# The S5 half of the first output projection moved into attention, two score areas instead of three, and a later turning and router

## What the reference computes

```python
s = jnp.einsum('bqhcd,bkhcd->bchqk', q_blk, k) * scale
p = jax.nn.softmax(jnp.where(mask, s, NEG_INF), axis=-1)
w = p[:, 0] - lam * p[:, 1]
return jnp.einsum('bhqk,bkhe->bqhe', w, v)
...
return jnp.concatenate([y_s5, y_da], axis=-1) @ w_out.astype(F32)
```

## Time and profile before

| what | value |
|---|---|
| median of three runs | 2639.55 us (2636.16 to 2640.43) |
| the profiled execution | 2635.27 us, of which the span of the profile is 2633.5 us |
| TensorE (PE) busy | 2322.1 us, 88% |
| VectorE (DVE), ScalarE (ACT), GpSimd (POOL) busy | 824.5, 495.9, 312.3 us |
| attention | from about 351 to 572 us |
| projection of layer 0 | from 572.4 to 732.7 us |
| projection of layer 1 | from 1772.1 to 1965.6 us |

### The profile page before, as it was taken

How to read it: one execution, slowest core, us unless ns; L and a number is a source line. 1 busy time by engine, 2 the same in 40 slices (tenths; PEclk the granted TensorE clock), 3 DMA queues, 4 the chain that set the end, 5 groups by cost and what they waited for, 6 DMA issues and landing times. The chain is left out here.

```text
span 2633.5 us, 33884 instructions
## 1 busy us (share of the span) xinstructions
PE 2322.1 (88%) x13631; PEld 1319.5 (50%) x13631; DVE 824.5 (31%) x1648; ACT 495.9 (19%) x910; POOL 312.3 (12%) x267
## 2 busy tenths in 40 slices
PE   6999978889949999999966999969976999999975
PEld 4787545555445445444524666634544445545432
DVE  5642135552241111111143555552233101111116
ACT  2222123431100000000012444430110000000002
POOL 6252000001101101111021000001100111111002
PEclk9999977899969999999977999989987999999997
DMA  4000010010269989998845111101019998999965
GB/s 142 34 33 14 3 66 1 1 36 32 81 242 419 414 352 409 414 411 354 358 170 161 36 36 36 36 17 35 25 72 357 419 413 336 409 412 370 411 248 210
DMA packets 142119, 528.42 MB, mean 201 GB/s; under 512 B 38128, under 2 KB 61200, under 8 KB 125584
## 3 DMA queue, kind: packets, MB, share of 16 engines
q1 hardware_dynamic: 115696, 465.70, 45.1%
q0 software_dynamic: 13600, 40.65, 4.0%
q10 hardware_dynamic: 12672, 19.95, 2.3%
HBM read 492.24 MB, written 40.57 MB: 202 GB/s over the span
## 5 line engine op out<-in xcount | busy, mean ns | idle before, releaser
L1644 PE MATMUL l_main_pgu<-l_w_ring,l_ex_xT 128*64 128x256 f32 (+1 forms) x4992 | 489.2, 385 | 13.7 <-DMA l_w_ring<-in_l_moe_w_gate 11.6
L1644 PEld LDWEIGHTS l_main_pgu<-l_w_ring,l_ex_xT 128*64 128x64 f32 (+1 forms) x4992 | 294.3, 130 | 198.7 <-issue 40.6
L1690 PE MATMUL l_main_py<-l_w_ring,l_ex_hT 128*64 128x512 f32 (+1 forms) x1248 | 239.3, 595 | 1.6 <-DVE l_ex_hT L1749 1.6
L1641 PE MATMUL l_main_pgu<-l_w_ring,l_ex_xT 128*128 128x512 f32 x384 | 178.2, 620 | 23.5 <-DMA l_w_ring<-in_l_moe_w_gate 23.5
L1041 PE MATMUL l_po<-w_out,y1T 128*128 128x512 f32 (+1 forms) x360 | 160.2, 601 | 17.7 <-PEq L2178 17.7
L1749 DVE COPY l_ex_hT<-l_main_ph 128x256 f32<-128x256 f32 (+1 forms) x78 | 36.3, 465 | 422.4 <-PE l_main_ph L1665 422.4
L2043 PE MATMUL lru_pr<-h2T,lru_wz 128*128 128x352 f32 (+1 forms) x480 | 143.7, 460 | 9.7 <-DMA lru_wax<-in_l_lru_w_x 9.7
L1745 DVE TENSOR_TENSOR l_ex_hid<-l_ex_sil,l_main_pgu 128x256 f32<-128x256 f32 (+1 forms) x78 | 36.0, 462 | 350.2 <-PE l_main_pgu L1644 268.8
L2048 PE MATMUL lru_pg<-h2T,lru_wz 128*128 128x352 f32 (+1 forms) x480 | 141.5, 455 | 0.0
L1690 PEld LDWEIGHTS l_main_py<-l_w_ring,l_ex_hT 128*64 128x64 f32 (+1 forms) x1248 | 71.5, 128 | 136.6 <-issue 129.6
L1641 PEld LDWEIGHTS l_main_pgu<-l_w_ring,l_ex_xT 128*128 128x128 f32 x384 | 74.5, 198 | 116.5 <-issue 88.4
(11 more groups left out here) (410 smaller groups left out, 2798.9 us busy)
## 6 DMA issues: line engine op xcount, KB each, us to landing
l_w_ring<-in_l_moe_w_gate SPq DMA_DIRECT2D x64, 2048.0 KB, 23.6
l_w_ring<-in_l_moe_w_up SPq DMA_DIRECT2D x64, 2048.0 KB, 21.1
l_w_ring<-in_l_moe_w_down SPq DMA_DIRECT2D x64, 2048.0 KB, 22.6
l_y<-expert_rows ACTq DMA_DIRECT2D x32, 512.0 KB, 5.5
h_rows<-H SPq DMA_DIRECT2D x24, 512.0 KB, 4.6
lru_wz<-in_l_w_in SPq DMA_DIRECT2D x20, 512.0 KB, 5.0
w_in<-in_l_w_in SPq DMA_DIRECT2D x3, 2048.0 KB, 8.0
w_out<-in_l_w_out SPq DMA_DIRECT2D x2, 2560.0 KB, 14.7
```

The lines of the kernel that those rows point to most:

```text
L1641: last = pe.matmul(out[:], x[:, k, :], w[0][:, k, :], start=k == 0, stop=k == KD - 1)
L1644: last = pe.matmul(out[HALF * h + o:HALF * h + o + m, 0:256], x[:, k, it.at + o:it.at + o + m], w[n][:, k, 256 * h:256 * h + 256], start=k ...
L1690: last = pe.matmul(py[b][HALF * h + o:HALF * h + o + m, :], hT[:, c % 2, HALF * (c // 2) + o:HALF * (c // 2) + o + m], ws[n][:, c, 512 * h ...
```

## The change

In `attention`, the three score areas become two, one for each component, and the two PSUM banks that this frees hold partial output tiles. At step `u` TensorE makes, right behind `scores(u+1)`, half of a half tile of the S5 part of the projection (`partial(u-2)`: two products of 512 columns). Every second step VectorE adds the residual to a finished half tile and writes it to `K.H` (`keep_part`). SP loads the residual tiles in attention. `scores(u)` now waits for both exponentials of the unit before. The buffers of probabilities are two pairs instead of three.

In `project_and_norm`, layer 0 has only its four attention products left and adds them to `K.H`. In both layers `turn` runs two tiles and `router` three tiles behind the products, ScalarE's copies stand behind its part of the norm, and the constants of `route` stand in VectorE's step 3.

```diff
-    PROBS, LAG = 3, 2
+    PROBS, LAG = 2, 2
...
-        S = [ctx.enter_context(nc.psum_tensor(f"scores{i}", [P, WIDE], F32)) for i in range(3)]
+        S = [ctx.enter_context(nc.psum_tensor(f"scores{i}", [P, WIDE], F32)) for i in range(2)]
+        part = [ctx.enter_context(nc.psum_tensor(f"out_part{i}", [P, 512], F32)) for i in range(2)]
...
             load_w_out(sp, K, 0)
+            for i in range(NT):
+                if i >= 2:
+                    sp.wait_ge(part_used, 2 * (i - 1))
+                load_rows(sp, res[i % 2], residual, i, res_loaded[i % 2])
...
                 if u:
-                    pe.wait_ge(exp_done, 2 * u - 1)
+                    pe.wait_ge(exp_done, 2 * u)
...
-                    place = lambda c, a, b: S[(2 * u + c) % 3][0:m, a:b]
+                    place = lambda c, a, b: S[c][0:m, a:b]
...
+            def partial(n):
+                i, h, k0 = n // 4, n // 2 % 2, 2 * (n % 2)
+                t0, m = TILES[i]
+                f = n // 2
+                if n == 0:
+                    pe.wait_ge(w_loaded, 32)
+                if f >= 2 and k0 == 0:
+                    pe.wait_ge(part_used, f - 1)
+                for k in (k0, k0 + 1):
+                    last = pe.matmul(part[f % 2][0:m, :], K.yT[:, k, t0:t0 + m], w_out[:, k, 512 * h:512 * h + 512], start=k == 0, stop=k == 3)
+                if k0:
+                    last.then_inc(part_ready, 1)
+
             for u in range(-1, U + LAG):
                 if u + 1 < U:
                     scores(u + 1)
+                if u >= LAG:
+                    partial(u - LAG)
                 for j in range(max(groups)):
...
+            def keep_part(f):
+                i, h = f // 2, f % 2
+                m, c = TILES[i][1], slice(512 * h, 512 * h + 512)
+                dve.wait_ge(part_ready, f + 1)
+                dve.wait_ge(res_loaded[i % 2], 16 * (i // 2 + 1))
+                dve.scalar_tensor_tensor(out=K.H[0:m, i, c], in0=res[i % 2][0:m, c], scalar=ALPHA, in1=part[f % 2][0:m, :], op0=ALU.mult, op1=ALU.add).then_inc(part_used, 1)
...
                     square(u - LAG - 1)
+                if u >= LAG + 1 and (u - LAG) % 2:
+                    keep_part((u - LAG) // 2)
...
-            for i in range(NT + 2):
+            for i in range(NT + 3):
                 if i < NT:
                     if i >= 2:
                         pe.wait_ge(z_done, 2 * (i - 1))
                     output(i, 0)
-                if i >= 2:
-                    router(i - 2)
+                if i >= 3:
+                    router(i - 3)
                 if i < NT:
                     output(i, 1)
-                if 1 <= i <= NT:
-                    turn(i - 1)
+                if 2 <= i < NT + 2:
+                    turn(i - 2)
...
-            for i in range(NT + 1):
-                if i >= 1:
...
-                if i < NT:
-                    norm.act(act, i)
+            for i in range(NT + 2):
+                if i < NT:
+                    norm.act(act, i)
+                if i >= 2:
+                    m = TILES[i - 2][1]
+                    act.wait_ge(turned, i - 1)
...
-            K.route_constants.dve(dve, do, consts)
-            for i in range(NT + 2):
+            for i in range(NT + 3):
...
+                            dve.tensor_tensor(K.H[0:m, i, c], K.H[0:m, i, c], po[i % 2][h][0:m, :], ALU.add).then_inc(z_done, 1)
...
-                if i >= 2:
-                    m = TILES[i - 2][1]
-                    if i == 2:
+                if i >= 3:
+                    m = TILES[i - 3][1]
+                    if i == 3:
+                        K.route_constants.dve(dve, do, consts)
                         dve.wait_ge(r_loaded, 7 * 16)
-                    dve.wait_ge(lg_ready, i - 1)
+                    dve.wait_ge(lg_ready, i - 2)
...
+    attention(nc, K, A, rows0)
+    K.end_phase()
+    project_and_norm(nc, K, A, 0, [K.daT[:, k, :] for k in range(HEADS)], 4, Place(nc, K.free_loop), None)
```

More of the change, by code:

```diff
@@ L630, in _, with attention @@
                 pool.sem_inc(h_ready, 1)
-def attention(nc, K, A):
-    at, top = Place(nc, K.free_loop), Place(nc, K.h_at)
-    K.daT = at("daT", [HEADS, T])
-    K.free_da = at.at
-    PROBS, LAG = 3, 2
+def attention(nc, K, A, residual):
+    at = Place(nc, K.free_loop)
+    K.daT = Place(nc, K.free_yT)("daT", [HEADS, T])
+    PROBS, LAG = 2, 2
     probs = [[at(f"prob{b}{c}", [T]) for c in range(2)] for b in range(PROBS)]
-    w = [top(f"w_rows{i}", [T]) for i in range(2)]
+    w = [at(f"w_rows{i}", [T]) for i in range(2)]
     wT = [at(f"w_cols{i}", [NT, P]) for i in range(2)]
@@ L649, in attention @@
     sq, ss, rs, g = at("o_sq", [2, P]), at("o_ss", [NT, HEADS]), at("o_rs", [NT, HEADS]), at("subln", [1])
+    o_sb, res = at("o_rows", [NT, 512]), [at(f"l0_res{i}", [D]) for i in range(2)]
     assert at.at <= K.w_out0_at
-    o_sb = top("o_rows", [NT, 512])
+    w_out, w_loaded = K.w_out[0], K.w_out_loaded[0]
     sem = lambda n: K.sem("da_" + n)
     (loaded, hide_made, lam_ready, lexp_done, s_ready, mn_ready, exp_done, w_ready, turned, turned_a, turned_v, o_ready, o_copied,
-     squared, dve_order, tail_done, tail_made) = map(sem, (
+     squared, dve_order, tail_done, tail_made, part_ready, part_used) = map(sem, (
         "loaded", "hide_made", "lam_ready", "lexp_done", "s_ready", "mn_ready", "exp_done", "w_ready", "turned", "turned_a",
-        "turned_v", "o_ready", "o_copied", "squared", "dve_order", "tail_done", "tail_made"))
+        "turned_v", "o_ready", "o_copied", "squared", "dve_order", "tail_done", "tail_made", "part_ready", "part_used"))
+    res_loaded = [sem("res_loaded0"), sem("res_loaded1")]
     ms_ready, sd_ready, on_ready, oT_ready, oT_copied, g_ready = map(sem, ("ms_ready", "sd_ready", "on_ready", "oT_ready", "oT_copied", "g_ready"))
@@ L993, in load_w_out, with project_and_norm @@
         sp.dma_start(w[:, :, 512 * c:512 * c + 512], src[:, :, 512 * c:512 * c + 512]).then_inc(loaded, 16)
-def project_and_norm(nc, K, A, layer, slices, at, residual):
+def project_and_norm(nc, K, A, layer, slices, k0, at, residual):
     L = f"l{layer}"
     ns = len(slices)
-    res = [at(f"{L}_res{i}", [D]) for i in range(2)]
+    res = [at(f"{L}_res{i}", [D]) for i in range(2)] if residual else None
     hT, wr, rb = at(L + "_h1T", [KD, P]), at(L + "_w_router", [KD, 36]), at(L + "_b_router", [36])
@@ L1024, in _ @@
                 sp.dma_start(rb[:, GROUPS:36], A[L + "_moe_b_fine"].rearrange("(a g) e -> a (g e)", a=1).to_broadcast([P, NE])).then_inc(r_loaded, 16)
-            for i in range(NT):
+            for i in range(NT if residual else 0):
                 if i >= 2:
@@ L1040, in output @@
                 for k, y in enumerate(slices):
-                    last = pe.matmul(po[i % 2][h][0:m, :], y[:, t0:t0 + m], w_out[:, k, 512 * h:512 * h + 512], start=k == 0, stop=k == ns - 1)
+                    last = pe.matmul(po[i % 2][h][0:m, :], y[:, t0:t0 + m], w_out[:, k0 + k, 512 * h:512 * h + 512], start=k == 0, stop=k == ns - 1)
                 last.then_inc(o_ready, 1)
@@ L1096, in _ @@
                         dve.wait_ge(o_ready, 2 * i + h + 1)
-                        dve.scalar_tensor_tensor(out=K.H[0:m, i, c], in0=res[i % 2][0:m, c], scalar=ALPHA, in1=po[i % 2][h][0:m, :],
-                                                 op0=ALU.mult, op1=ALU.add).then_inc(z_done, 1)
+                        if residual:
+                            dve.scalar_tensor_tensor(out=K.H[0:m, i, c], in0=res[i % 2][0:m, c], scalar=ALPHA, in1=po[i % 2][h][0:m, :],
+                                                     op0=ALU.mult, op1=ALU.add).then_inc(z_done, 1)
+                        else:
+                            dve.tensor_tensor(K.H[0:m, i, c], K.H[0:m, i, c], po[i % 2][h][0:m, :], ALU.add).then_inc(z_done, 1)
                     dve.wait_ge(z_done, 2 * i + 2)
@@ L1102, in _ @@
                     norm.apply_gain(dve, i)
-                if i >= 2:
-                    m = TILES[i - 2][1]
-                    if i == 2:
+                if i >= 3:
+                    m = TILES[i - 3][1]
+                    if i == 3:
+                        K.route_constants.dve(dve, do, consts)
                         dve.wait_ge(r_loaded, 7 * 16)
-                    dve.wait_ge(lg_ready, i - 1)
-                    dve.tensor_tensor(K.logits[0:m, i - 2, :], pl[0:m, :], rb[0:m, :], ALU.add).then_inc(lg_done, 1)
+                    dve.wait_ge(lg_ready, i - 2)
+                    dve.tensor_tensor(K.logits[0:m, i - 3, :], pl[0:m, :], rb[0:m, :], ALU.add).then_inc(lg_done, 1)
             dve.wait_ge(lg_done, NT)
@@ L2214, in hybrid_block_kernel @@
     K.end_phase()
-    attention(nc, K, A)
-    K.end_phase()
     x, meta = A["x"].rearrange("a b d -> (a b) d"), A["meta"]
     rows0 = lambda i: meta if i == 0 else x[P * (i - 1):P * i, :]
-    slices = [K.yT[:, k, :] for k in range(4)] + [K.daT[:, k, :] for k in range(HEADS)]
```

(6 more changed lines are left out.)

10 lines of the change are left out of this document (5 added, 5 removed).

## The result

The changed kernel took 2647.58 us (median of 11 runs, 2643.87 to 2655.66), the one before 2636.16 in the same series (11 runs, 2629.95 to 2640.43). The medians are 11.4 us apart. The ratio of the two series is 1.0047, with a 95% interval of 1.0035 to 1.0059, which is 12.4 us: slower, and clear of the noise. The profiled execution after took 2648.27 us, its span 2646.5 against 2633.5.

The account below looks back on a forecast made before the run. TensorE was taken to bound layer 0's projection, and to be busy 80 to 84% in attention at a clock of 0.80 to 0.84. 40 - 38.6 + 7.7 = +9 us on 2639.55 gave 2648.5, range 2630 to 2665.

Parts of the forecast that it names:

- Attention, +40 forecast: Attention with the added products and two score areas: 50 us longer less 10 for the clock, between +28 and +53.
- the wait for the second exponential: Attention: in 18 units the next scores wait 0.25 to 1.84 us for the unit's second exponential, 22.4 us in all.
- the parts in units where TensorE has no room: Attention: 13 units, small ones or next to a wide one, where the extra products of 1.71 us cost 21 us.
- gave 10 back by the clock: Attention: the parts fill gaps, so scores run at full clock; at most 18 us, taken as 10.
- my first rival: Dense products raise attention's clock and 25 us come back: 9 us faster, 2630.5 us; chance 0.24.
- the signs of being wrong: Projection tiles of 9.5 us, attention under +30, or a clock above 0.95 in attention.
- Layer 0's projection, -38.6 forecast: 50.5 us less up to the last product, 6.5 more at the end, and 2.4 and 3 for slower clock.
- my clock term: Layer 0's projection: +2.4 us behind the 6 us gap before `router(1)`, and 3 for five gaps of 1.8 us.
- my sum of tiles: Layer 0's projection: tile 4's products end at 45.7 us, then four more tiles at 11.3 us, to 90.9.
- The end, +6.5 a layer: Behind each projection's last product, router, turning and copy come once more at the lower clock: 6.5 us.
- layer 1's term: Layer 1's projection: constants push the logits in step 3, +1.2 us, and the end grows by 6.5: together +7.7.
- The wait for `w_out`, 0 (to 3) forecast: Attention: `partial(0)` waits for `w_out`, landing 13.4 us after 353.5, with the fourth scores ending at 368: 0 to 3 us.

Follow-up runs that it names:

- e1: The kernel before with two score areas, two pairs of probabilities and the scores' wait for both exponentials, without the partial products: 2668.09 us, ratio 1.0139.
- e2: The kernel before with only the changed order in the projections (later turning and router, copies behind the norm, constants in the fourth step): 2649.92 us, ratio 1.0062.
- e3: The changed kernel with the constants of route back ahead of the loop: 2633.79 us, ratio 0.9996 to the kernel before.
- e5: e4 with VectorE adding the bias to the logits ahead of the norm's statistics: 2605.68 us, ratio 0.9885 to the kernel before.
- e11: e10 with ScalarE's copies of the turned tile ahead of its part of the norm: 2592.32 us, ratio 0.9841 to the kernel before.
- e10: The changed kernel with constants in front, logits ahead of the statistics, and attention's second minimum and copies ahead of combining: 2613.24 us, ratio 0.9919.
- e7: e5 and e6 together, in one kernel with the half inside attention: 2590.29 us, ratio 0.9833 to the kernel before.
- e8: The kernel before, half still in the projection, with logits ahead of the statistics and both minima ahead of combining: 2615.28 us, ratio 0.9914.
- e4: The changed kernel with the projections' old order (turning one tile behind, router two, copies ahead of the norm, constants in front): 2630.97 us, ratio 0.9987.
- e6: The changed kernel with VectorE's second minimum and copies ahead of combining in attention: 2632.57 us, ratio 0.9995 to the kernel before.
- e9: The changed kernel with the constants in the same step but ahead of the norm's statistics: 2643.02 us, ratio 1.0028 to the kernel before.

## Why the prediction was right, and which of its terms were not

The sign was right, and so was the time, 2648.5 forecast and 2647.6 measured. That these are within 1 us is luck in part: I forecast 9 us over a median of 2639.55 from three runs, and the change is 11.4 us over the 2636.16 of eleven. By stages it is 14.1 where I had 9.1, with -2.1 in a stretch that nothing touches. The terms:

- *Attention, +40 forecast, +37.4 measured.* The sum held; its parts didn't. I put 22.4 us on the wait for the second exponential, 21 on the parts in units where TensorE has no room, and gave 10 back by the clock. e1 shows the wait at 34 us by itself, half of it as slower clock, and the parts at 3 net. That these errors cancelled is luck. What failed is the treatment of the clock as a correction at the end: it works on each term. The idle time that e1 adds, 16.6 us, is even under the 22.4; the 17.4 of slower clock that comes with it was not in the term. Against before, TensorE's busy time grew by 46.5 us for 61.7 us of work, so the clock gave 15.2, and the idle time shrank by 9.5. The Trainium skill, "TensorE: Matmul & The Clock Gate", section "What's actually happening", has the direction right: the default is the lower clock and activity lifts it; the trace agrees at both ends, 0.72 without the parts and 0.90 with them. The 15.2 were not enough for my first rival, which decides from 21 us on. One of the signs of being wrong came up in part: the window from 400 to 450 us had 0.97, above the 0.95 that I named, the stage as a whole 0.90.
- *Layer 0's projection, -38.6 forecast, -31.8 measured* (122 us forecast, 128 measured). The structure is as worked out: tile 3's products ended 29.97 us in (forecast 29.9), one long wait in front of `router(1)`, a wait of 1.77 in each tile (1.8). Three sizes were off: the constants took 6.0 us beside GpSimd's addition instead of 4.3 (1.8 over); the router and products behind the long wait ran slow for 4.4 us, not 2.4; the four gaps (my clock term counted five, my sum of tiles four) cost 5.1 us of clock and not 3, and a tile is 11.55 instead of 11.3 (1.0). Together that is 6.9 us, and 6.8 were missed.
- *The end, +6.5 a layer.* The rows at the end of the stage are as forecast. The turning and router which move there are missing from the products' phase, -2.6 (e2): layer 0's sum, tile by tile, has that, layer 1's term left it out. There it was made up by the constants: 4.5 us, a wait of 2.7 and 1.8 of slower clock, instead of the 1.2 that I took. So +8.5 there, forecast 7.7, is right by two errors.
- *The wait for `w_out`, 0 (to 3) forecast.* `partial(0)` waited 0.50 us for it.

What the prediction didn't ask is whether the projections' waits belong to what was changed or to the place of three small things in two queues. They are such places: the constants (e3, 13.8 us), the logits' addition (e5, 25.3), ScalarE's copies (e11 against e10, 20.9). With them mended, moving the half is worth 20 to 25 us (e7 against e8) and the later order of turning and router nothing either way (e11 against e7). Nor did it split the change in its two parts: the half alone gains 3 us (e4) and the order with the constants in the loop costs 16 (e2), so the loss is not the price of the move.

Not settled: how much of e6's gain is the minimum and how much the copies, which it moves together; and why the clock differs between kernels with the same attention code. Their idle time agrees within 1.4 us; the 3.6 and 7.3 us by which attention differs are TensorE's busy time at a granted clock of 0.90 to 0.93.

## What to carry to other kernels

When work is taken out of a loop that TensorE bounds, list what each other engine still has between two of its results that TensorE needs, in the order of its queue: here an addition of 0.19 us behind a norm of 5 us, a copy of 1.05 behind a scaling, and a table made in the loop decided whether the move of the half comes with a loss of 12 us or a gain of 20 to 25. Put the instruction that frees or feeds TensorE first in its queue, since whoever computes for the tile after next can wait. And price a wait on TensorE at up to twice its length where it leaves gaps in each unit: in e1, 16.6 us of idle time brought 17.4 us of slower clock with them, in e8 6.3 us less gave 6.7 back, but e6's edit, with 8.5 less, gave only some 2 back on the mean of the kernels that have it, where the clock was 0.90 before.

## What the runs showed of the hardware

- A VectorE addition on 128x1 with both inputs in SBUF took 1.90 us while GpSimd's addition on 128x1024 ran, and ended with it; 0.15 us when GpSimd was idle (e9). The three TENSOR_SCALAR operations on 128x1 right in front of it, beside the same addition of GpSimd, took their usual 0.14 to 0.15 us. The Trainium skill names this contention in "GPSIMD Engine Reference", section "Specifications": the SBUF interfaces are shared with VectorE, with contention for instructions with two SBUF inputs. The trace agrees.
- Gaps of 1.77 us, one in each tile of 11.5 us with TensorE busy in the rest, were followed by products at the lower clock behind three of four of them (after: 5.36 to 5.38 us against 3.68), and gaps of 1.20 to 1.21 us by the same behind three of five in e10 (4.97 to 5.38). Without the gaps the same stage ran at 0.99 (e11, 597 to 680 us).
